# MLP block 0's preparation moved from the start of the MLP into the merge's output rounds

## The reference, cut to what matters

```python
# merge: three branches o_b, gates from the input projection
x = x + (sum_b sigmoid(G_b) * (o_b @ W_br[b])) @ W_out
# MLP: 1,024 -> 4,096 -> 1,024
u = _rmsnorm(x, norm2)                 # x * rsqrt(mean(x*x) + 1e-6) * norm2
x = x + jnp.square(jax.nn.relu(u @ W1)) @ W2
y = _rmsnorm(x, norm_f)
```

## Time and profile before

| | |
|---|---|
| three runs, median | 3136.56 us (3135.22 to 3141.76) |
| profiled execution, its own time | 3140.97 us |
| its span, first to last instruction | 3139.3 us |
| mean granted clock of TensorE | 0.982 |
| TensorE matmul busy | 3008.3 us, 96% |
| VectorE / ScalarE / GpSimd busy | 1332.2 / 1139.2 / 1150.3 us |
| first instruction of the MLP block | 2053.45 us into the span |

### The profile page before, as it was taken

One profiled execution on the slowest core, in us unless ns is written; L12 is line 12 of the kernel. 1 busy time (PEld: TensorE's weight loads), 2 busy tenths in 40 slices (PEclk: granted clock), 3 DMA queues, 4 the chain that ended last, 5 costly groups with the idle time before them and its releaser, 6 DMA issues. The chain is left out here.

```text
span 3139.3 us, 44169 instructions
## 1 busy us (share of the span) xinstructions
PE 3008.3 (96%) x17907; PEld 2454.4 (78%) x17907; DVE 1332.2 (42%) x1933; ACT 1139.2 (36%) x1907; POOL 1150.3 (37%) x753
## 2 busy tenths in 40 slices
PE   5999999999999969899998999979999999999998
PEld 4878787878887746788886887868888888888887
DVE  4233232312379869667665343122224232322323
ACT  4241413243134349567664112232332323233232
POOL 4221121211111040033110433456666666666764
PEclk8999999999999979999999999989999999999999
DMA  4434232433445266111103544333323233333331
GB/s 111 164 137 128 75 116 82 141 102 116 161 144 168 107 222 208 66 52 35 60 22 103 166 160 165 98 124 94 99 90 107 82 106 121 94 94 94 102 119 62
DMA packets 239593, 353.14 MB, mean 112 GB/s; under 512 B 32928, under 2 KB 186272, under 8 KB 239392
## 3 DMA queue, kind: packets, MB, share of 16 engines
q1 hardware_dynamic: 239392, 350.32, 34.4%
HBM read 263.71 MB, written 96.36 MB: 115 GB/s over the span
## 5 line engine op out<-in xcount | busy, mean ns | idle before, releaser
L102 PE MATMUL pj_acc<-u_hi,pj_w_hi 128*128 128x512 f32 x1464 | 582.9, 398 | 13.1 <-POOL u_lo L532 13.1
L2448 DVE TENSOR_TENSOR x_tm<-m_ps,x_tm 128x512 f32<-128x512 f32 x384 | 264.9, 691 | 744.2 <-PE m_ps L104 744.2
L104 PE MATMUL pj_acc<-u_hi,pj_w_lo 128*128 128x512 f32 x1464 | 571.8, 391 | 0.0
L103 PE MATMUL pj_acc<-u_lo,pj_w_hi 128*128 128x512 f32 x1464 | 571.2, 390 | 0.0
L526 POOL TENSOR_TENSOR pj_w_lo<-pj_w_raw,pj_w_hi 128x1024 fp32r<-128x1024 f32 x61 | 157.8, 2588 | 817.4 <-ACT pj_w_hi L560 817.4
L102 PEld LDWEIGHTS pj_acc<-u_hi,pj_w_hi 128*128 128x128 f32 x1464 | 275.9, 188 | 91.3 <-issue 22.0
L2325 POOL TENSOR_TENSOR m_w_lo<-m_w_raw,m_w_hi 128x1024 fp32r<-128x1024 f32 x96 | 237.8, 2501 | 263.2 <-ACT m_w_hi L2239 263.2
L103 PEld LDWEIGHTS pj_acc<-u_lo,pj_w_hi 128*128 128x128 f32 x1464 | 276.1, 189 | 59.6 <-issue 3.8
L104 PEld LDWEIGHTS pj_acc<-u_hi,pj_w_lo 128*128 128x128 f32 x1464 | 275.6, 188 | 58.5
L102 PE MATMUL m_ps<-m_v_hi,m_w_hi 128*128 128x512 f32 x768 | 299.6, 390 | 2.4 <-DVE m_v_lo L2416 2.4
L102 PE MATMUL m_ps<-m_w_hi,m_h_hi 128*128 128x512 f32 x768 | 299.5, 390 | 0.0
(11 more groups left out here) (278 smaller groups left out, 5239.1 us busy)
## 6 DMA issues: line engine op xcount, KB each, us to landing
m_w_raw<-in_w_mlp_dram SPq DMA_DIRECT2D x48, 1024.0 KB, 5.4
m_w_raw<-in_w_mlp_dram SPq DMA_DIRECT2D x96, 512.0 KB, 3.6
proj<-pj_stage SPq DMA_DIRECT2D x61, 768.0 KB, 3.5
pj_w_raw<-in_w_in_dram SPq DMA_DIRECT2D x61, 512.0 KB, 4.9
mo_gate<-proj SPq DMA_DIRECT2D x24, 768.0 KB, 4.3
mo_w_raw<-in_w_out_dram SPq DMA_DIRECT2D x48, 256.0 KB, 2.6
rpb_bias<-pj_shut SPq DMA_DIRECT2D x48, 192.0 KB, 3.0
rpb_bias<-rpb_near SPq DMA_DIRECT2D x24, 384.0 KB
```

The costliest lines, as they stand in the source:

```text
L102: pe.matmul(out, w_hi, x_hi, start=first, stop=False)
L103: pe.matmul(out, w_hi, x_lo, start=False, stop=False)
L104: return pe.matmul(out, w_lo, x_hi, start=False, stop=last)
L2448: dve.tensor_tensor(xt, ps2[:, q % 4], xt, ALU.add).then_inc(added, 1)
```

## The change

Block 0's preparation is issued from the merge block. The four hi/lo buffers of the MLP (tokens, W1, W2) now lie in the merge's `held` and `m_lo`/`total`, whose parts are free once a token block's rounds are over; the raw weights lie in `gate`, `xn` and the gains in `oz`, as before. The class `MlpViews` holds these views.

- SP loads the gains in its iteration (1,0), the first up-weights in (2,0), the first down-weights in (2,2) and (2,4), the second up-weights in (5,0), the last after a wait for two low halves.
- ScalarE: the squares in slots (2,1) to (2,4), the root in (2,6), the high halves of the tokens in (3,2), (3,4), (3,6), (4,2), those of the first four up-weight tiles in (4,4), (4,6), (5,4), (5,6).
- VectorE, behind the additions of a round: statistics and two normalizations after round 1's, low halves of the tokens and the other two normalizations after round 2's, the rest of the low halves after rounds 3 and 4. The low halves of these up-weights are VectorE's now; GpSimd made them before.
- TensorE: the four turns after slots (3,1), (3,3), (3,5) and (4,1), into PSUM banks 2 to 5.
- The MLP's own code for block 0 is replaced by increments of the semaphores that it would have counted; it begins with the split of the down-weights and the first up.

```diff
@@ -1840,7 +1840,37 @@
...
+class MlpViews:
+    def __init__(self, held, m_lo, gate, spare, stats):
+        self.hi, self.lo = held, m_lo
+        raw = gate[:].rearrange("p a n -> p (a n)")
+        self.v_hi, self.v_lo = held[:, :, 0:TB], m_lo[:, :, 0:TB]
+        self.w1_raw = raw[:, 0:2 * D].rearrange("p (k n) -> p k n", k=KD)
+        self.w2_raw = raw[:, 2 * D:4 * D].rearrange("p (j n) -> p j n", j=2)
+        self.xn, self.g2, self.gf = spare[:, 0:2 * D].rearrange("p (b n) -> p b n", b=2), spare[:, 2 * D:3 * D], spare[:, 3 * D:4 * D]
+        self.ss, self.ms, self.rr, self.rstd = (stats[:, n] for n in range(4))
+    def w1_hi(self, m):
+        return self.hi[:, :, TB + m % 4 * P:TB + (m % 4 + 1) * P]
+    def w1_lo(self, m):
+        return self.lo[:, :, TB + m % 4 * P:TB + (m % 4 + 1) * P]
+    def w2_hi(self, m):
+        return self.hi[:, 2 * (m % 4):2 * (m % 4) + 2, 2 * TB:3 * TB]
+    def w2_lo(self, m):
+        return self.lo[:, 2 * (m % 4):2 * (m % 4) + 2, 2 * TB:3 * TB]
...
@@ -1857,12 +1887,12 @@
...
     with Space(nc, "mo") as s:
-        held = s.sb("held", [2 * KB, T], F32R)
-        m_lo, total = s.over("m_lo", "total", [KD, T], F32R, F32)
+        held, m_lo, total, gate, stats = shared
+        spare = oz[:].rearrange("p a n -> p (a n)")
+        first = MlpViews(held, m_lo, gate, spare, stats)
...
         w_hi, w_lo = s.sb("w_hi", [2, TB], F32R), s.sb("w_lo", [2, TB], F32R)
-        gate = s.sb("gate", [3, T])
...
@@ -1878,6 +1908,20 @@
...
         SPREAD_AT = {2: (0, 1), 3: (2,)}
...
+        SQUARE_AT = {(2, 1 + j): j for j in range(TPB)}
+        ROOT_AT = (2, 6)
+        TURN_AT_SLOT = {(3, 1): 0, (3, 3): 1, (3, 5): 2, (4, 1): 3}
+        HIGH_V_AT = {(3, 2): 0, (3, 4): 1, (3, 6): 2, (4, 2): 3}
+        HIGH_W1_AT = {(4, 4): 0, (4, 6): 1, (5, 4): 2, (5, 6): 3}
+        w1_t = w1.rearrange("(k p) n -> p k n", p=P)
+        def turn_bank(j):
+            return ps[:, 2 + 2 * (j % 2):4 + 2 * (j % 2)].rearrange("p a (k n) -> p (a k) n", n=P)
...
@@ -1976,6 +2020,22 @@
...
                     sp.dma_start(x_tm[:, t], rows[t]).then_inc(x_in[t], 16)
+                if (rd, c) == (1, 0):
+                    for buf, v in ((first.g2, gain2), (first.gf, gainf)):
+                        sp.dma_start(buf, v.rearrange("(a n) -> a n", a=1).to_broadcast([P, D])).then_inc(gain_in, 16)
+                if (rd, c) == (2, 0):
+                    sp.wait_ge(gated, MS)
+                    sp.dma_start(first.w1_raw, w1_t[:, :, 0:2 * P]).then_inc(w1_in, 16)
+                if rd == 2 and c in (2, 4):
+                    j = c // 2 - 1
+                    sp.dma_start(first.w2_raw[:, j], w2[j * P:(j + 1) * P, :]).then_inc(w2_in[j], 16)
+                if (rd, c) == (5, 0):
+                    sp.wait_ge(w1_lo_done, 2)
+                    sp.dma_start(first.w1_raw, w1_t[:, :, 2 * P:4 * P]).then_inc(w1_in, 16)
...
@@ -2016,6 +2076,27 @@
...
                     high_m(KD - 1)
+                at_slot = (rd, c)
+                if at_slot in SQUARE_AT:
+                    j = SQUARE_AT[at_slot]
+                    act.wait_ge(added, TPB + j + 1)
+                    if j:
+                        act.wait_ge(squared, j)
+                    else:
+                        act.wait_ge(last_out, 16)
+                    act.activation(first.xn[:, j % 2], x_tm[:, j], ACT.Square, accum_out=first.ss[:, j:j + 1]).then_inc(squared, 1)
+                if at_slot == ROOT_AT:
+                    act.wait_ge(recip, 1)
+                    act.activation(first.rstd[:, 0:TPB], first.rr[:, 0:TPB], ACT.Sqrt).then_inc(rooted, 1)
+                if at_slot in HIGH_V_AT:
+                    j = HIGH_V_AT[at_slot]
+                    act.wait_ge(turned, j + 1)
+                    act.copy(first.v_hi[:, :, j * P:(j + 1) * P], turn_bank(j)).then_inc(v_hi_done, 1)
+                if at_slot in HIGH_W1_AT:
+                    m = HIGH_W1_AT[at_slot]
+                    act.wait_ge(w1_in, 16 * (m // 2) + 16)
+                    act.wait_ge(out_done, 4 * TPB)
+                    act.copy(first.w1_hi(m), first.w1_raw[:, :, m % 2 * P:(m % 2 + 1) * P]).then_inc(w1_hi_done, 1)
...
@@ -2082,6 +2163,14 @@
...
                         last.then_inc(slot_done, 1)
+                if (rd, c) in TURN_AT_SLOT:
+                    j = TURN_AT_SLOT[(rd, c)]
+                    pe.wait_ge(normed, j + 1)
+                    if j >= 2:
+                        pe.wait_ge(v_lo_done, j - 1)
+                    for k in range(KD):
+                        last = pe.transpose(turn_bank(j)[:, k], first.xn[:, j % 2, k * P:(k + 1) * P], ident[:])
+                    last.then_inc(turned, 1)
...
@@ -2128,6 +2217,21 @@
...
             low_m(KD - 1)
+            def normal(j):
+                if j >= 2:
+                    dve.wait_ge(turned, j - 1)
+                dve.scalar_tensor_tensor(first.xn[:, j % 2], x_tm[:, j], first.rstd[:, j:j + 1], first.g2, ALU.mult, ALU.mult).then_inc(normed, 1)
+            def low_v(j):
+                dve.wait_ge(v_hi_done, j + 1)
+                sl = slice(j * P, (j + 1) * P)
+                dve.tensor_tensor(first.v_lo[:, :, sl], turn_bank(j), first.v_hi[:, :, sl].bitcast(F32), ALU.subtract).then_inc(v_lo_done, 1)
+            def low_w1(m):
+                dve.wait_ge(w1_hi_done, m + 1)
+                dve.tensor_tensor(first.w1_lo(m), first.w1_raw[:, :, m % 2 * P:(m % 2 + 1) * P], first.w1_hi(m).bitcast(F32),
+                                  ALU.subtract).then_inc(w1_lo_done, 1)
...
@@ -2136,10 +2240,33 @@
...
                     dve.tensor_tensor(xt, out(t), xt, ALU.add).then_inc(added, 1)
+                if rd == 1:
+                    dve.wait_ge(gain_in, 32)
+                    dve.wait_ge(squared, TPB)
+                    dve.tensor_scalar(first.ms[:, 0:TPB], first.ss[:, 0:TPB], 1.0 / D, EPS, ALU.mult, ALU.add).then_inc(meaned, 1)
+                    dve.wait_ge(meaned, 1)
+                    dve.reciprocal(first.rr[:, 0:TPB], first.ms[:, 0:TPB]).then_inc(recip, 1)
+                    dve.wait_ge(rooted, 1)
+                    normal(0)
+                    normal(1)
+                if rd == 2:
+                    for j in range(3):
+                        low_v(j)
+                        if j < 2:
+                            normal(j + 2)
+                if rd == 3:
+                    low_v(3)
+                    low_w1(0)
+                    low_w1(1)
+                if rd == 4:
+                    low_w1(2)
+                    low_w1(3)
             dve.wait_ge(added, RND * TPB)
...
+            dve.wait_ge(v_lo_done, TPB)
+            dve.wait_ge(w1_lo_done, 4)
...
@@ -2188,14 +2308,16 @@
...
         def _(sp):
-            sp.dma_start(g2, gain2.rearrange("(a n) -> a n", a=1).to_broadcast([P, D])).then_inc(gain_in, 16)
-            sp.dma_start(gf, gainf.rearrange("(a n) -> a n", a=1).to_broadcast([P, D])).then_inc(gain_in, 16)
+            sp.sem_inc(gain_in, 32)
+            sp.sem_inc(w1_in, 32)
+            for b in range(2):
+                sp.sem_inc(w2_in[b], 16)
...
                 g = gg % NG
...
@@ -2268,13 +2387,10 @@
...
                 act.copy(v_hi[:, :, j * P:(j + 1) * P], turn_bank(bk, j)).then_inc(v_hi_done, 1)
-            for j in range(TPB):
-                square(0, j, j)
-            root(0, 0, TPB, 1)
-            high_w1(0)
-            for j in range(TPB):
-                high_v(j)
-            high_w1(1)
+            act.sem_inc(squared, TPB)
+            act.sem_inc(rooted, 1)
+            act.sem_inc(v_hi_done, TPB)
+            act.sem_inc(w1_hi_done, 4)
...
@@ -2420,13 +2534,10 @@
...
             dve.wait_ge(gain_in, 32)
-            mean(0, 0, TPB, 1, TPB)
-            dve.wait_ge(rooted, 1)
-            for j in range(TPB):
-                normal(j)
-                if j:
-                    low_v(j - 1)
-            low_v(TPB - 1)
+            dve.sem_inc(meaned, 1)
+            dve.sem_inc(recip, 1)
+            dve.sem_inc(normed, TPB)
+            dve.sem_inc(v_lo_done, TPB)
...
```

More of the change, by code:

```diff
@@ L1880, in merge_project @@
         SPREAD_AT = {2: (0, 1), 3: (2,)}
+        (gain_in, w1_in, w1_hi_done, w1_lo_done, squared, meaned, recip, rooted, normed, turned, v_hi_done, v_lo_done) = (
+            s.sem(f"first_{x}") for x in ("gain_in", "w1_in", "w1_hi_done", "w1_lo_done", "squared", "meaned", "recip", "rooted",
+                                          "normed", "turned", "v_hi_done", "v_lo_done"))
+        w2_in = [s.sem(f"first_w2_in{b}") for b in range(2)]
+        SQUARE_AT = {(2, 1 + j): j for j in range(TPB)}
[6 more added lines that the diff above has]
+            return ps[:, 2 + 2 * (j % 2):4 + 2 * (j % 2)].rearrange("p a (k n) -> p (a k) n", n=P)
         block = s.block()
@@ L2154, in mlp @@
     with Space(nc, "m") as s:
[L2155 to L2158, removed]
+        w1_raw, w2_raw, v_hi, v_lo, xn, g2, gf = (views.w1_raw, views.w2_raw, views.v_hi, views.v_lo, views.xn, views.g2, views.gf)
```

(18 more changed lines are left out.)

29 lines of the change are left out of this document (13 added, 16 removed).

## The result

The changed kernel takes 3141.16 us (median of 20 executions, 3137.61 to 3145.0), the one before 3136.53 in the same series. The ratio is 1.0014 (95% interval 1.0007 to 1.002): 4.6 us slower, which is clear of the spread but inside the 0.2% called "no change", and outside the predicted range. Two of the twenty executions of the kernel before stand far out (3404.08 and 9298.33 us); without them its median is 3136.30. The profiled span is 3142.8 us instead of 3139.3.

The account below looks back on a forecast made before the run. TensorE, busy nearly throughout, was taken as the bound: only matmul time and its idle stretches move the end. 21.7 + 0 - 3.6 - 0.35 = 17.75 us gained, so 3136.56 becomes 3118.8 us, range 3115.0 to 3124.5.

Parts of the forecast that it names:

- What it adds on TensorE: In merge rounds 3 and 4, four turns of 8 transposes add 3.6 us, bounds 3.2 to 5.4.
- own signs of being wrong: Wrong if merge round 1, 2 or 3 grows over 4 us besides turns, or the MLP's start still waits.
- Removed, 21.7 us: At the merge-MLP edge, the first up product starts at 2053.75 instead of 2075.46, saving 21.7 us (21.0 to 21.9).
- Turns, 0.90 us each: Each group of 8 transposes between merge slots of rounds 3 and 4 costs TensorE 0.90 us.
- The stop at round 3, 0.35 us: Normalizations delay GpSimd's subtraction in slot (2,7), so TensorE stops 0.25 us and restarts with 0.1 more; bounds 0 and 1.6.
- DMAs, 0: Added loads on SP's queue delay no merge weight: cost 0, with 0.6 us at each of two places as far end.
- Rival B: Port collisions or late transfers stall merge rounds 1 to 3 by 1.3 to 3 us; gain 13 to 16 us; chance 0.22.
- The clock, 0: After the edge's 2.24 us pause the clock drops as before, losing the same 1.74 us: difference 0.
- rival A: The clock holds 2.4 GHz after the short edge pause: 1.6 us more, 19.4 us gained, 3117.2 us; chance 0.22.
- Rival C: GpSimd's MLP splits into strided views take 4.1 us and bound the kernel: slower, 3143 us; chance 0.03.
- Rival D: The MLP's first product finds another late thing, leaving some 3 us of gain, 3133 us; chance 0.04.

Follow-up runs that it names:

- e1: The changed kernel with the 384-byte statistics tile removed and the statistics kept in free columns of `gate`: 3116.88 us, ratio 0.9938 to the kernel before.
- e4: The changed kernel with the statistics tile padded from 384 to 512 bytes: 3117.68 us, ratio 0.9938 to the kernel before.
- e2: The kernel before the change with an unused 384-byte tile between the operands' tiles in merge and MLP: 3159.46 us, ratio 1.0071.
- g1: The changed kernel with 128 unused bytes ahead of the MLP's `rel` and hidden tiles, restoring only the down products' offset: 3127.07 us, ratio 0.996 to the kernel before.
- f1: The kernel before the change with pads shifting merge operands by 256 bytes, up by 64 and down by 128: 3159.25 us, one execution.
- f3: The kernel before the change with pads shifting merge operands by 64 bytes, up by 256 and down by 448: 3143.14 us, one execution.

## Why the prediction was wrong

**The step that failed** is the part "What it adds on TensorE". The prediction named matmul time as one of the two things that move the end, and then counted for it the turns alone (3.6 us) and took the 227 ns of every product as unchanged. The sum had no term for the tiles that move, and gave no reason for that. With 1,440 merge products x 5.8 ns = 8.4 us (5.8 is the mean of 5.6 and 6.1 in the table, weighted by 864 branch and 576 output products) and 2,304 down products x 5.7 ns = 13.1, it would have been 17.75 - 21.5 = -3.8, that is 3140.3; 3141.16 was measured. The two runs that take this cause away with the rest of the change in place (e1, e4), and the one that adds it without the change (e2), show it from both sides; g1 takes away the MLP's part alone. That e1 and e4 (3116.88 and 3117.68 us) fall into the predicted range says that the rest of the sum was sound.

The merge's +11.1 us come out too: 8.4 for the product distance, 3.5 for four turns and 0.2 for the stop at round 3 (both below), less 1.0 of pauses that were a little shorter than before (at the merge's start 10.4 instead of 11.2, at its output rounds 2.6 instead of 2.8).

The prediction's own signs of being wrong did not show. No round became longer by more than 4 us besides the turns (96 products x 6.1 ns are 0.6 us), and the MLP's start waits for nothing after the edge. They looked at the places where the change adds or removes work; the loss is spread thinly over 3,744 products.

**Removed, 21.7 us: right.** 24.34 - 2.82 = 21.5, and in e1 the edge takes 2.82 too.

**Turns, 0.90 us each: right.** TensorE around one of them:

```profile
1998.21 0.40 PE L104 MATMUL mo_ps<-mo_w_hi,m_lo 128*128 128x512 f32 x1
1998.45 1.03 PE L2172 MATMUL mo_ps<-ident,oz 128*128 128x128 f32 x8
1999.24 0.48 PE L102 MATMUL mo_ps<-mo_w_hi,held 128*128 128x512 f32 x1
1999.56 0.39 PE L103 MATMUL mo_ps<-mo_w_lo,held 128*128 128x512 f32 x1
```

1.35 us where two starts take 0.47: 0.88.

**The stop at round 3, 0.35 us: right in place and kind.** VectorE's two normalizations took 3.50 us together, GpSimd's subtraction behind them 1.92 instead of 1.29, and ScalarE's next casts stand 3.02 us apart instead of 2.81; in e1 3.15 instead of 2.72. So the stop is 0.2 us in the changed kernel and 0.4 in e1.

```profile
1988.03 3.50 DVE L2224 SCALAR_TENSOR_TENSOR oz<-x_tm,stats,oz 128x1024 f32<-128x1024 f32 x2 [4.02 <-ACT stats L2090]
...
1990.77 1.92 POOL L2105 TENSOR_TENSOR mo_w_lo<-mo_w_raw,mo_w_hi 128x512 fp32r<-128x512 f32 x1 [1.51 <-ACT mo_w_hi L2046]
...
1992.88 0.62 ACT L2046 CAST mo_w_hi<-mo_w_raw 128x512 fp32r<-128x512 f32 x1 [2.19 <-PE mo_ps L104]
```

**DMAs, 0: right for the changed kernel's profile, but close.** The merge's weight loads issued between 1944 and 2000 us landed in 2.5/3.4/6.2 us (shortest, median, longest), the longest just at the lead of 6.2, and no cast in those rounds waits for one. In the profiles of e1, e4 and g1 the longest took 7.0, 6.8 and 6.9 us, and three casts waited for a load in each. The longest such wait in e1, and the one stop of TensorE behind it:

```profile
1946.33 0.62 ACT L2046 CAST mo_w_hi<-mo_w_raw 128x512 fp32r<-128x512 f32 x1 [2.83 <-DMA mo_w_raw<-in_w_out_dram]
...
1948.37 0.50 PE L102 MATMUL mo_ps<-mo_w_hi,held 128*128 128x512 f32 x1 [0.30 <-POOL mo_w_lo L2105]
```

The starts around it are 0.69 and 0.33 us apart instead of 0.23 twice, so 0.6 us are lost, which is the far end that the prediction gave for one place. Rival B (late transfers) occurs there, well under its 1.3 to 3 us.

**The clock, 0: a step that a single row could not decide.** The prediction placed 2.24 us of pause between one that kept 1.00 and one of 2.77 that fell to 0.67. But the same pause went both ways. Here is the granted clock (the number before the last two) in the 5 us after the edge, where TensorE had paused for 2.42 or 2.43 us. First the kernel after:

```profile
2065.80:2070.80 5.00, 4.92 (x14) 3.87 (x15) 0.00 (x0) 1.99 (x2) 3.63 (x2) 0.66 0.09 15
```

In e1, at the edge and then after the pause of 2.77 us before the output rounds:

```profile
2053.00:2058.00 5.00, 4.91 (x21) 4.05 (x22) 0.00 (x0) 2.00 (x2) 3.61 (x2) 1.00 0.05 8
1920.53:1925.53 5.00, 5.00 (x22) 4.11 (x23) 0.00 (x0) 1.19 (x2) 2.44 (x2) 1.00 0.35 107
```

In e4, at the edge; at its output rounds it was 0.66 too, after the same 2.77 us, as in the kernel before:

```profile
2056.00:2061.00 5.00, 4.84 (x14) 3.84 (x15) 0.00 (x0) 1.99 (x2) 3.53 (x2) 0.66 0.10 11
```

At each place 7 starts lie between the two cases in the same 5 us, that is 1.6 us. So forecast and rival A were not two theories but one case, with a chance between them for each execution. With two such places, e1's profile is some 3.2 us better than e4's by this alone. The medians of e1 and e4 lie 20.2 and 19.4 us under the 3137.03 beside them, and their executions spread over 5.6 and 7.5 us: that cannot tell the 17.75 of the forecast from the 19.4 of rival A.

**Rival C (0.03, slower by the layout)** had the direction of the result, and its 3143 us lie within 2 of the time measured, but that is luck: its place is wrong. GpSimd's splits over the strided views take as long as before, 2500 and 2399 ns (the other line, L2434) against 2501 and 2395:

```profile
L2441 POOL TENSOR_TENSOR m_lo<-gate,held 128x1024 fp32r<-128x1024 f32 x96 | 237.9, 2500 | 282.3 <-ACT held L2358 282.3
```

It looked at what the views do to the engine that writes them, and not at what the new addresses do to the engine that reads them. **Rival D** (0.04, some 3 us gained) foresaw the class of the outcome, "within 0.2%", but neither its sign nor its cause: nothing late was found at the MLP's start.

## What to carry to other kernels

When a change adds or drops even a small tile, list the addresses of every product's two operands before and after, and for products like these (128x128 by 512 columns) keep their distance a multiple of 256 bytes: a pad of 128 bytes gave back 13 us of the MLP here. After any change compare the distance of matmul starts in the stages that were not meant to change, since neither the list of waits nor the chain shows a matmul that merely starts 6 ns later. A gain read from a wait that vanished is real only when the stretches around it kept their length.

## What was not expected of the hardware

The products with 512 columns start 226.7 ns apart at best, and every shift tried that is no multiple of 256 bytes cost something: 32, 128 and 384 bytes 5.5 to 6.7 ns (2.4 to 3%); 64 bytes 6.4 ns where the stationary operand was shifted and 2.3 to 2.9 where it was the moving one, and 448 bytes the other way round, 2.1 to 2.2 and 6.5. These fit together if 448 is read as 64 the other way: what counts then is how far the stationary operand lies from the moving one, modulo 256. Shifts of 256 and 512 bytes were free (one stage at 256 had 227.4), and none was faster. Offsets between those tried, other shapes of product, and why the chip does this, stay open. The other thing is the clock: pauses of 2.43 and of 2.77 us, with the same work around them, were followed by 1.2 GHz in some executions and by the full clock in others (e1 at both places; f1 and f3 too at the output rounds, after 2.77 and 2.62 us, with a granted clock of 1.00).
